# Clearing the expert row tables as attention begins instead of as the dense layer begins

## The chip, the cores and the metric

The kernel runs on one core of one Trainium2 chip. The metric is the device time of one execution in microseconds (us). Beside the time there is a profile of one execution, whose span runs from its first to its last instruction.

## What is computed

A decoder trunk of two layers on 256 tokens of width 1024. Layer 0 is gated DeltaNet linear attention and a dense SwiGLU (width 2816). Layer 1 is sliding-window attention with 16 query heads, 4 key/value heads and a learned sink per head, then a top-2-of-8 SwiGLU mixture of experts. After each of the four parts comes `layer_norm(ALPHA*x + h)`. What matters here, from the reference:

```python
    m = jnp.maximum(jnp.max(s, axis=-1, keepdims=True), sink)
    p = jnp.exp(s - m)
    p = p / (jnp.sum(p, axis=-1, keepdims=True) + jnp.exp(sink - m))
...
    top_v, top_i = lax.top_k(logits, TOP_K)
    top_w = jax.nn.softmax(top_v, axis=-1)
    gates = jnp.sum(jax.nn.one_hot(top_i, N_EXPERTS, dtype=jnp.float32) * top_w[..., None], axis=1)
    out = jnp.zeros_like(xt)
    for e in range(N_EXPERTS):
        h = xt @ w_gu[e]
        y = (jax.nn.silu(h[:, :D_EXPERT]) * h[:, D_EXPERT:]) @ w_down[e]
        out = out + gates[:, e:e + 1].astype(xt.dtype) * y
```

So attention needs the sinks for its very first maximum, and each expert works on the rows that the router sends to it.

## The kernel before, in words

The program is written engine by engine; each engine runs its list in order, and semaphores tie the lists together. The order within a list is the order of the code. The tokens are two blocks of 128.

**Weights.** All big weights pass as units of 1 MB (128 partitions x 2048 float32). SP loads unit j in two halves into one of six buffers `raw`, as soon as VectorE has cut unit j-6. ScalarE makes `hi` (a rounded copy, `cut_hi`, line 572), VectorE makes `lo = raw - hi` (`cut_lo`, line 946), and TensorE multiplies with both parts (most of it recorded as line 1529). The cuts run three units ahead of use. The units come in the order dense gate and up (U_GU), dense down (U_DOWN), shared key/value (U_KV), queries (U_Q), attention output (U_O), experts (U_MOE).

**The row tables.** `xe` and `ys` are tables in DRAM. For the experts, `xe` takes the rows of x sent to each expert by an indirect store, and `ys` their results; both have rows that nobody writes and that must be zero, so both are cleared once. Source of the zeros is `xTf[:, 0:4, :]`, an SBUF buffer set to zero by POOL (line 481). It gets its real content, the transposed x for the router, only behind the third norm: ScalarE's `xT_copy` and VectorE's `turned_sum` (line 1329).

**POOL's list around the change.** Behind the first norm (`norm(0)`): constants, the memset of xTf, the four clears (lines 484 to 487), more constants, then the small loads `wr` (router weights) and `gbT` (norm vectors). Then `norm(1)`, the norm behind the dense layer, which ends with the loads of `lng` and `lnb` (lines 397, 398). Then the memsets of `kT2` (lines 500, 501), the load of the sinks `sk` (line 503), the distances `dist`, and `wgb = wr * gbT` (line 515), for which a TensorE product in the midst of the key/value projection waits. All DMAs that POOL issues go through one queue of its own, q0; SP's go through q1.

**Attention.** TensorE alternates query projections and score products: queries(0), half of queries(1), scores(0), half of queries(1) and (2), scores(1), and so on. `scores(gi)` of TensorE waits for `sc_bias` gi, which VectorE's `scores(gi-1)` raises when it has taken the products out of PSUM. ScalarE's `exps` follow, then VectorE's `probs`, which TensorE transposes (line 1887). Ahead of its first `cut_lo` and `scores(0)` VectorE waits for the sinks and the distances:

```python
            dve.wait_ge(sink_here, 16)
            dve.wait_ge(consts, 4)
...
            cut_lo(U_Q + 0 + AHEAD)
            scores(0)
            cut_lo(U_Q + 1 + AHEAD)
            scores(1)
            probs(0)
```

`cut_lo(U_Q + 0 + AHEAD)` cuts unit U_Q+3. Behind attention the third norm follows, the router, and the experts. POOL waits for `xe_clear` before it stores rows in `xe`, and for `ys_clear` before the experts' results are gathered.

Of the kernel before, what the change touches and what calls it, by code (L numbers as in the profile page):

```python
# [25 lines left out]
P = 128  # L26
# [9 lines left out]
def trunk(nc, x_in, w_in, conv_w, a_log, dt_bias, norm_w, w_out, w_kv, w_q, sinks, w_o, w_gu, w_down,  # L36
          w_router, moe_gu, moe_down, ln_g, ln_b, out):
    _, T, D = x_in.shape
    NB = T // P
    KD = D // P  # L40
# [10 lines left out]
    E = w_router.shape[2]  # L51
# [24 lines left out]
    with ctx:  # L76
        def sb(name, shape, dt=F32, where=None):
            return (where or ctx).enter_context(nc.sbuf_tensor(name, shape, dt))

        def sem(name):  # L80
            return ctx.enter_context(nc.semaphore(name))
# [100 lines left out]
        xTf = sb("xTf", [P, KD, T])  # L182
# [66 lines left out]
        oneh_here, row_here, xe_clear, dispatched = (sem(n) for n in ("oneh_here", "row_here", "xe_clear", "dispatched"))  # L249
        gathered, xg_turned, xg_hi_here, xg_here = (sem(n) for n in ("gathered", "xg_turned", "xg_hi_here", "xg_here"))  # L250
        silu_here, act_here, ff_turned, h_hi, h_here = (sem(n) for n in ("silu_here", "act_here", "ff_turned", "h_hi", "h_here"))
        ys_clear = sem("ys_clear")
# [20 lines left out]
        xe = nc.dram_tensor("xe", [E * 2 * P, D], F32).ap()  # L273
        ys = nc.dram_tensor("ys", [E * 2 * P + P, D], F32).ap()
        NO_ROW = E * 2 * P
        xe_v = xe.rearrange("(e q s) d -> q e s d", q=2, s=P)
        ys_v = ys[0:NO_ROW, :].rearrange("(e q s) d -> q e s d", q=2, s=P)
# [12 lines left out]
        def xT_part(buf, s):  # L290
            return buf[:, 4 * (s % 2):4 * (s % 2) + 4, (s // 2) * P:(s // 2) * P + P]
# [81 lines left out]
        def _(pool):  # L373
            n = [0]

            def link(ins):
                n[0] += 1
                ins.then_inc(pool_chain, 1)
# [17 lines left out]
            def load_ln(layer, i):  # L396
                pool.dma_start(lng[:, :], ln_g[layer, i].partition_broadcast(P)).then_inc(ln_here, 16)
                pool.dma_start(lnb[:, :], ln_b[layer, i].partition_broadcast(P)).then_inc(ln_here, 16)
# [25 lines left out]
            def rsqrt(dst, src):  # L424
                return pool.tensor_tensor(dst, src, mhalf[:, 0:src.shape[1]], ALU.pow)  # L425
# [3 lines left out]
            for gr in range(4):  # L429
                s = slice(4 * gr, 4 * gr + 4)  # L430
# [3 lines left out]
            for gr in range(4):  # L434
                s = slice(4 * gr, 4 * gr + 4)
# [12 lines left out]
            for gr in range(4):  # L448
                s = slice(4 * gr, 4 * gr + 4)
# [17 lines left out]
            def norm(i):  # L467
                for b in range(NB):
                    pool.wait_ge(ln_var, 2 * i + b + 1)
                    rsqrt(lnrs[:, b:b + 1], lnve[:, b:b + 1]).then_inc(ln_rstd, 1)  # L470
                if i < 3:
                    pool.wait_ge(ln_done[0], i + 1)
                    pool.wait_ge(ln_done[1], i + 1)
                    load_ln((i + 1) // 2, (i + 1) % 2)
# [6 lines left out]
            link(pool.memset(xTf[:, 0:4, :], 0.0))  # L481
            settle()
            zeros = xTf[:, 0:4, :].rearrange("p k t -> p (k t)").unsqueeze(1)
            pool.dma_start(xe.rearrange("(r s) d -> s r d", s=P), zeros.to_broadcast([P, 2 * E, D])).then_inc(xe_clear, 16)
            pool.dma_start(ys_v[1].rearrange("e s d -> s e d"), zeros.to_broadcast([P, E, D])).then_inc(ys_clear, 16)
            pool.dma_start(ys[NO_ROW - 2 * P:NO_ROW - P, :], xTf[:, 0:4, :].rearrange("p k t -> p (k t)")).then_inc(ys_clear, 16)
            pool.dma_start(ys[NO_ROW:NO_ROW + P, :], xTf[:, 0:4, :].rearrange("p k t -> p (k t)")).then_inc(ys_clear, 16)
            link(pool.memset(last_place[:, :], float(P)))
            select(last_place[:, :], ALU.is_ge, 0.0, E - 2, [[-1, E]], 0)
            link(pool.iota(first_row[:, :], [[2 * P, E]], base=-1 - NO_ROW, channel_multiplier=0, allow_small_or_imprecise_dtypes=True))  # L490
# [4 lines left out]
            settle()  # L495
            pool.sem_inc(consts, 1)
            norm(1)


            link(pool.memset(kT2[64:128, :, 0, :], 0.0))  # L500
# [3 lines left out]
            for c, (base, op) in enumerate(((0, ALU.is_ge), (P, ALU.is_gt), (0, ALU.is_ge))):  # L504
                d = dist[:, c * P:(c + 1) * P]
# [61 lines left out]
        def _(act):  # L567
# [9 lines left out]
            def copy(dst, src, scale=1.0):  # L577
                return act.activation(dst, src, ACT.Copy, scale=scale)  # L578
# [74 lines left out]
            for gr in range(4):  # L653
                s = slice(4 * gr, 4 * gr + 4)
# [41 lines left out]
            for q in range(4, 4 * 7):  # L696
                s = slice(4 * (q % 4), 4 * (q % 4) + 4)
# [136 lines left out]
            def xT_copy(i):  # L834
                act.wait_ge(turned, 16 + i + 1)
                copy(xT_part(xTf, i), ps[:, 4 + i, :].rearrange("p (k t) -> p k t", k=4)).then_inc(xT_act, 1)

            xT_copy(0)
            xT_copy(1)
            act.wait_ge(xT_act, 2)  # L840
# [88 lines left out]
        def _(dve):  # L929
# [14 lines left out]
            def cut_lo(j, it=0):  # L944
                dve.wait_ge(hi_ready, j + 1 + PER_IT * it)
                dve.tensor_tensor(slot(lo, j), slot(raw, j), slot(hi, j).bitcast(F32), ALU.subtract).then_inc(lo_ready, 1)  # L946
# [156 lines left out]
            for gr in range(4):  # L1103
                s = slice(4 * gr, 4 * gr + 4)
# [6 lines left out]
            for gr in range(4):  # L1111
                s = slice(4 * gr, 4 * gr + 4)
# [212 lines left out]
            attended(3)  # L1325
            cut_lo(U_O + 1 + AHEAD)
            def turned_sum():
                dve.wait_ge(turned, 19)
                dve.tensor_copy(xT_part(xTf, 2), ps[:, 6, :].rearrange("p (k t) -> p k t", k=4)).then_inc(xT_dve, 1)
                dve.wait_ge(turned, 20)  # L1330

            norm(2, 0, U_O + 3, risen=turned_sum)

            each = [P, NB, E]
# [810 lines left out]
```

## Time and profile before

| | |
|---|---|
| median of 3 runs | 1269.55 us (1268.96 to 1269.56) |
| span of the profiled execution | 1267.7 us |
| TensorE (PE) busy | 1242.9 us, 98% |
| VectorE (DVE) busy | 1003.8 us, 79% |
| ScalarE (ACT) busy | 834.6 us, 66% |
| GpSimd (POOL) busy | 101.7 us, 8% |
| moved by DMA | 375.75 MB, mean 296 GB/s |

The profiled execution's own time is not among the three; its span stands 1.85 us below their median, and the start and end of an execution lie in that difference. Busy shares are means over stages with different limits. TensorE's end times are modelled. "Idle before" in a timeline names what the instruction waited for last.

### The profile page before, as it was taken

How to read it: one execution, taken by the hardware profiler on the slowest of the kernel's cores; microseconds unless marked ns; L12 is line 12 of the kernel's file. 1: busy time of each engine (PE TensorE's matmuls, PEld its weight loads, DVE VectorE, ACT ScalarE, POOL GpSimd, SP SyncE). 2: the span in 40 equal slices, each digit the busy share in tenths (PEclk: the TensorE clock that was granted, in tenths of full speed). 3: DMA queues.
4: the chain of work that ended last, by engine and by line, in shares of the span. 5: the costliest groups of instructions: out<-in, count | busy, mean ns of one | idle time of the engine just before them, and what ended most of it. 6: DMA issues, size and time to landing. Idle time of an engine off the chain costs nothing.

```text
span 1267.7 us, 16828 instructions
## 1 busy us (share of the span) xinstructions
PE 1242.9 (98%) x6731; PEld 1060.1 (84%) x6731; DVE 1003.8 (79%) x868; ACT 834.6 (66%) x842; POOL 101.7 (8%) x120
## 2 busy tenths in 40 slices
PE   9999999999999999999999999999999999999995
PEld 8998998888888978888888888888888888888884
DVE  6877846556646677988888888888888988898897
ACT  6795344545534474777777777777777777778773
POOL 4044212000001001300000000000000000001100
PEclk9999999999999999999999999999999999999998
DMA  9834013997554514999999999999999999999991
GB/s 315 271 148 137 2 34 125 413 348 243 181 186 163 192 43 166 333 397 397 389 393 389 390 384 371 391 388 372 389 387 377 386 391 378 382 380 363 390 397 74
DMA packets 189060, 375.75 MB, mean 296 GB/s; under 512 B 12321, under 2 KB 69777, under 8 KB 188977
## 3 DMA queue, kind: packets, MB, share of 16 engines
q1 hardware_dynamic: 179888, 345.02, 75.1%
q0 software_dynamic: 6928, 25.82, 5.4%
q10 hardware_dynamic: 2160, 3.79, 0.8%
q8 instruction: 55, 0.90, 0.3%
q14 instruction: 29, 0.23, 0.1%
HBM read 354.13 MB, written 20.45 MB: 295 GB/s over the span
## 4 chain that ended last, share of the span: by engine, by line
PE 88%; DMA 5%; DVE 3%; ACT 2%; POOL 1%; issue 1%; SPq 0%; DVEq 0%; POOLq 0%; ACTq 0%
PE ps L1529 85%; DMA raw<-in_ffn_w_gu 2%; DMA raw<-in_moe_w_gu 2%; PE ps L2041 1%; ACT hi L572 1%; DVE lo L946 1%; ACT ps L587 0%; PE ps L2034 0%; PE ps L1887 0%; PE ps L1660 0%; DMA x<-in_x 0%; DVE xT_both L954 0%; POOL lnrs L425 0%; SPq L306 0%; DVE x L1502 0%
## 5 line engine op out<-in xcount | busy, mean ns | idle before, releaser
L946 DVE TENSOR_TENSOR lo<-raw,hi 128x2048 fp32r<-128x2048 f32 x326 | 744.9, 2297 | 183.0 <-ACT hi L572 182.0
L572 ACT ACTIVATE hi<-raw 128x2048 fp32r<-128x2048 f32 x326 | 625.5, 1919 | 298.1 <-PE ps L1529 260.7
L1529 PE MATMUL ps<-hi,xg_hi 128*128 128x512 f32 x704 | 278.0, 395 | 0.1
L1529 PE MATMUL ps<-hi,xg_lo 128*128 128x512 f32 x704 | 274.6, 390 | 0.0
L1529 PE MATMUL ps<-lo,xg_hi 128*128 128x512 f32 x704 | 274.2, 389 | 0.0
L1529 PE MATMUL ps<-xT_both,hi 128*128 128x256 f32 (+1 forms) x896 | 222.9, 328 | 4.4 <-DVE xT_both L954 2.5
L1529 PE MATMUL ps<-xT_both,lo 128*128 128x256 f32 x624 | 175.8, 282 | 0.0
L1529 PEld LDWEIGHTS ps<-xT_both,hi 128*128 128x128 f32 x896 | 151.4, 191 | 20.1 <-issue 2.9
L1529 PEld LDWEIGHTS ps<-hi,xg_hi 128*128 128x128 f32 x704 | 132.2, 188 | 28.7 <-DVE lo L946 1.5
L1529 PEld LDWEIGHTS ps<-hi,xg_lo 128*128 128x128 f32 x704 | 132.1, 188 | 28.1
L1529 PEld LDWEIGHTS ps<-lo,xg_hi 128*128 128x128 f32 x704 | 132.3, 188 | 26.4
L1529 PEld LDWEIGHTS ps<-xT_both,lo 128*128 128x128 f32 x624 | 119.3, 191 | 0.0
L1529 PE MATMUL ps<-hi,hE_hi 128*128 128x512 f32 x352 | 111.1, 396 | 0.0
L1529 PE MATMUL ps<-hi,hE_lo 128*128 128x512 f32 x352 | 108.9, 390 | 0.0
L1529 PE MATMUL ps<-lo,hE_hi 128*128 128x512 f32 x352 | 108.9, 390 | 0.0
L1529 PEld LDWEIGHTS ps<-lo,hE_hi 128*128 128x128 f32 x352 | 66.1, 188 | 14.0
L1529 PEld LDWEIGHTS ps<-hi,hE_lo 128*128 128x128 f32 x352 | 66.1, 188 | 14.0
L1529 PEld LDWEIGHTS ps<-hi,hE_hi 128*128 128x128 f32 x352 | 64.0, 188 | 13.4 <-issue 1.1
L532 POOL DMA_DIRECT2D xg<-xe x7 | 3.8, 539 | 505.3 <-PE ps L2034 497.8
L1059 DVE SCALAR_TENSOR_TENSOR conv<-ps,cw,conv 128x255 f32<-128x255 f32 (+2 forms) x72 | 29.1, 471 | 10.2 <-ACT conv L613 10.1
L425 POOL TENSOR_TENSOR lnrs<-lnve,mhalf 128x1 f32<-128x1 f32 x8 | 7.0, 875 | 360.9 <-ACT lnve L590 360.9
L578 ACT ACTIVATE conv<-ps 128x512 f32<-128x512 f32 (+1 forms) x28 | 15.4, 564 | 29.3 <-PE ps L1529 29.3
(315 smaller groups left out, 1249.3 us busy)
## 6 DMA issues: line engine op xcount, KB each, us to landing
raw<-in_moe_w_gu SPq DMA_DIRECT2D x352, 512.0 KB, 7.2
raw<-in_moe_w_down SPq DMA_DIRECT2D x176, 512.0 KB, 7.1
raw<-in_ffn_w_gu SPq DMA_DIRECT2D x44, 512.0 KB, 8.1
raw<-in_dn_w_in SPq DMA_DIRECT2D x32, 512.0 KB, 8.9
raw<-in_ffn_w_down SPq DMA_DIRECT2D x22, 512.0 KB, 4.0
xe<-xTf POOLq DMA_DIRECT2D x1, 8192.0 KB, 29.0
raw<-in_dn_w_out SPq DMA_DIRECT2D x8, 512.0 KB, 3.9
ys<-xTf POOLq DMA_DIRECT2D x1, 4096.0 KB, 40.3
```

The source lines that it names most:

```text
L425: return pool.tensor_tensor(dst, src, mhalf[:, 0:src.shape[1]], ALU.pow)
L532: pool.dma_start(xg[:, :], xe_v[p][e]).then_inc(gathered, 16)
L572: act.activation(slot(hi, j), slot(raw, j), ACT.Copy).then_inc(hi_ready, 1)
L578: return act.activation(dst, src, ACT.Copy, scale=scale)
L946: dve.tensor_tensor(slot(lo, j), slot(raw, j), slot(hi, j).bitcast(F32), ALU.subtract).then_inc(lo_ready, 1)
L1059: dve.scalar_tensor_tensor(out=conv[:, t, d:T], in0=ps[:, t % 4, 0:T - d], scalar=cw[:, w:w + 1], in1=conv[:, t, d:T], op0=ALU.mult, op1=A ...
L1529: return pe.matmul(dst, lhsT, rhs, start=start, stop=stop)
L2041: last = pe.transpose(ps[:, 6 + c % 2, m * P:(m + 1) * P], actE[:, c % 2, m * P:(m + 1) * P], ident[:, :])
```

## The change

The four DMAs that clear `xe` and `ys` leave their place behind the memset of xTf and are issued behind `norm(1)`. Since the zeros are then read from xTf much closer to its reuse, the two engines that write it wait for the clears first.

```diff
             link(pool.memset(xTf[:, 0:4, :], 0.0))
             settle()
             zeros = xTf[:, 0:4, :].rearrange("p k t -> p (k t)").unsqueeze(1)
-            pool.dma_start(xe.rearrange("(r s) d -> s r d", s=P), zeros.to_broadcast([P, 2 * E, D])).then_inc(xe_clear, 16)
-            pool.dma_start(ys_v[1].rearrange("e s d -> s e d"), zeros.to_broadcast([P, E, D])).then_inc(ys_clear, 16)
-            pool.dma_start(ys[NO_ROW - 2 * P:NO_ROW - P, :], xTf[:, 0:4, :].rearrange("p k t -> p (k t)")).then_inc(ys_clear, 16)
-            pool.dma_start(ys[NO_ROW:NO_ROW + P, :], xTf[:, 0:4, :].rearrange("p k t -> p (k t)")).then_inc(ys_clear, 16)
             link(pool.memset(last_place[:, :], float(P)))
...
             norm(1)
+            pool.dma_start(xe.rearrange("(r s) d -> s r d", s=P), zeros.to_broadcast([P, 2 * E, D])).then_inc(xe_clear, 16)
+            pool.dma_start(ys_v[1].rearrange("e s d -> s e d"), zeros.to_broadcast([P, E, D])).then_inc(ys_clear, 16)
+            pool.dma_start(ys[NO_ROW - 2 * P:NO_ROW - P, :], xTf[:, 0:4, :].rearrange("p k t -> p (k t)")).then_inc(ys_clear, 16)
+            pool.dma_start(ys[NO_ROW:NO_ROW + P, :], xTf[:, 0:4, :].rearrange("p k t -> p (k t)")).then_inc(ys_clear, 16)
...
+            act.wait_ge(xe_clear, 16)
+            act.wait_ge(ys_clear, 48)
             xT_copy(0)
             xT_copy(1)
...
             def turned_sum():
+                dve.wait_ge(xe_clear, 16)
+                dve.wait_ge(ys_clear, 48)
                 dve.wait_ge(turned, 19)
```

POOL's list from the end of `norm(0)` to the load of the sinks, with the waits; first what stands in the kernel before:

```order
L481 MEMSET xTf 128x1024
L484 DMA xe<-xTf 128x16x1024 [waits pool_chain]
L485 DMA ys<-xTf 128x8x1024
L486 DMA ys<-xTf 128x1024
L487 DMA ys<-xTf 128x1024
L488 MEMSET last_place 128x8
L385 AFFINE_SELECT last_place<-last_place 128x8 [waits pool_chain]
L490 IOTA first_row 128x8
L491 DMA wr<-in_moe_w_router 128x8x8
L493 DMA gbT<-in_ln_g 128x8x1
L494 DMA gbT<-in_ln_b 128x8x1
```

The four clears stand ahead of wr and gbT in POOL's list and in its queue. Now the changed kernel, POOL's list behind `norm(1)`:

```order
L397 DMA lng<-in_ln_g 128x1024 [waits ln_done1,ln_done0]
L398 DMA lnb<-in_ln_b 128x1024
L494 DMA xe<-xTf 128x16x1024
L495 DMA ys<-xTf 128x8x1024
L496 DMA ys<-xTf 128x1024
L497 DMA ys<-xTf 128x1024
L500 MEMSET kT 64x4x256
L501 MEMSET kT 64x4x256
L503 DMA sk<-in_sw_sinks 128x16 [waits pool_chain]
```

They now stand ahead of the memsets of kT2 and of sk; wr and gbT have no clears ahead of them any more.

VectorE's list in the changed kernel, where it waits for the sinks (its order is the one of before):

```order
L1267 COPY vB<-ps 128x512 [waits unit_used]
L1269 TENSOR_REDUCE wsum<-ps 128x16 [waits wsum_mm]
L1270 TENSOR_SCALAR wsum<-wsum 128x8 [waits dve_chain]
L948 TENSOR_TENSOR lo<-raw,hi 128x2048 [waits hi_ready,consts,sink_here]
L1282 SCALAR_TENSOR_TENSOR sS<-dist,ps 128x128 [waits sc_mm]
```

Nothing moved there; the wait for sk (`sink_here`) stands in front of the cut of U_Q+3 and of scores(0).

## Rows read from the trace of the kernel before

**Rows 1.** Head of the page.
```profile
span 1267.7 us, 16828 instructions
```
**Rows 2.** The chain that ended last, dense layer: start us, us, what.
```profile
233.94 29.68 DMA raw<-in_ffn_w_gu
```
**Rows 3.** Timeline of PE, dense layer: start us, us, instruction, idle before it.
```profile
267.94 0.50 PE L1529 MATMUL ps<-xT_both,hi 128*128 128x512 f32 x1 [1.90 <-DVE lo L946]
```
**Rows 4.** Stretches: length; busy us of PE, PEld, DVE, ACT, POOL; clock, DMA share, GB/s.
```profile
217.60:261.60 44.00, 44.00 (x256) 38.46 (x255) 23.75 (x19) 16.98 (x17) 6.23 (x10) 1.00 1.03 401
...
268.00:274.00 6.00, 6.00 (x25) 5.18 (x26) 5.62 (x6) 5.42 (x6) 0.00 (x0) 0.72 1.10 349
...
300.00:340.00 40.00, 40.00 (x233) 35.28 (x232) 25.99 (x22) 20.94 (x23) 0.00 (x0) 1.00 0.53 189
...
411.00:456.00 45.00, 43.90 (x367) 40.80 (x365) 33.79 (x61) 25.31 (x64) 3.78 (x8) 1.00 0.50 169
```
**Rows 5.** DMA issues: count, KB each, median us from issue to landing.
```profile
xe<-xTf POOLq DMA_DIRECT2D x1, 8192.0 KB, 29.0
ys<-xTf POOLq DMA_DIRECT2D x1, 4096.0 KB, 40.3
...
wr<-in_moe_w_router POOLq DMA_DIRECT2D x1, 32.0 KB, 41.6
...
gbT<-in_ln_b POOLq DMA_DIRECT2D x1, 4.0 KB, 42.2
sk<-in_sw_sinks POOLq DMA_DIRECT2D x1, 8.0 KB, 4.6
```
**Rows 6.** Timeline of POOL behind the first norm.
```profile
217.60 1.20 POOL L484 DMA_DIRECT2D xe<-xTf  x1 [0.30 <-POOL xTf L481]
...
220.75 0.14 POOL L488 MEMSET last_place<- 128x8 f32 x1
...
221.21 0.94 POOL L491 DMA_DIRECT2D wr<-in_moe_w_router  x1
...
223.03 0.88 POOL L494 DMA_DIRECT2D gbT<-in_ln_b  x1
```
**Rows 7.** Timeline of POOL behind the second norm.
```profile
408.20 0.95 POOL L500 MEMSET kT<- 64x1024 f32 x1
...
410.44 0.54 POOL L503 DMA_DIRECT2D sk<-in_sw_sinks  x1 [0.30 <-POOL kT L501]
...
414.86 0.55 POOL L515 TENSOR_TENSOR wgb<-wr,gbT 128x64 f32<-128x64 f32 x2 [0.18 <-POOL dist L385]
```
**Rows 8.** Timeline of PE: the wgb product, scores(1), first turned probabilities.
```profile
415.46 0.49 PE L1529 MATMUL ps<-wgb,ones 128*128 128x128 f32 x2 [1.10 <-POOL wgb L515]
...
438.16 2.22 PE L1529 MATMUL ps<-kT,qT 64*128 64x256 f32 x16
...
448.12 1.04 PE L1887 MATMUL ps<-ident,sS 128*128 128x128 f32 x8
```
**Rows 9.** Timeline of SP's DMA queue: a pair of loads, one unit.
```profile
426.06 0.89 SPq L306 DMA_DIRECT2D raw<-in_moe_w_gu  x2
```
**Rows 10.** Timeline of DVE, from the router's sums to the first probabilities.
```profile
426.99 0.17 DVE L1268 TENSOR_SCALAR wsum<-wsum 128x8 f32<-128x8 f32 x1
...
432.52 0.29 DVE L1280 SCALAR_TENSOR_TENSOR sS<-dist,ps 128x128 f32<-128x128 f32 x1
...
434.31 0.41 DVE L1282 SCALAR_TENSOR_TENSOR sS<-dist,ps 128x256 f32<-128x256 f32 x1
...
437.89 2.29 DVE L946 TENSOR_TENSOR lo<-raw,hi 128x2048 fp32r<-128x2048 f32 x1 [0.83 <-ACT hi L572]
...
440.42 0.29 DVE L1280 SCALAR_TENSOR_TENSOR sS<-dist,ps 128x128 f32<-128x128 f32 x1 [0.24 <-PE ps L1529]
...
445.91 1.22 DVE L1300 TENSOR_TENSOR sS<-sS,sinv 128x1024 f32<-128x1024 f32 x1
```
**Rows 11.** Timeline of ACT: the first copy into xTf.
```profile
490.47 1.06 ACT L578 ACTIVATE xTf<-ps 128x512 f32<-128x512 f32 x2
```

## The prediction

> **What bounds the kernel now.** I read the page first: a span of 1267.7 us [rows 1]. The chain of work that ended last is almost all TensorE, so only what makes TensorE stand or run at its lower clock costs time. I then looked for where a DMA stands in that chain. It does once in the dense layer: a load of ffn_w_gu that took 29.68 us to land, then the two cuts of that weight unit (ScalarE, then VectorE) [rows 2]. At its end TensorE stands for 1.90 us [rows 3]. That is much less than 29.68 us, because weights loaded ahead covered the rest. Afterwards the granted clock averages 0.72 over the next 6 us (part of it at 1.2 GHz instead of 2.4) [rows 4]. In the undisturbed dense layer TensorE is busy throughout and weights come at 189 GB/s; during the clears the core moves 401 GB/s in all; in attention only 169 GB/s [rows 4].
>
> The clears are 8192 and 4096 KB [rows 5] and two of 128 x 1024 float32, 512 KB each: 13.63 MB. Over 44.0 us the core moved 17.6 MB, so only some 4.0 MB, about 90 GB/s, was left for weights, half of what the dense layer needs. The stall is the clears' doing.
>
> **What is removed.** Without clears the dense layer keeps its 189 GB/s. The standing time goes, 1.90 us, and so does the loss by the clock, (1 - 0.72) x 6 = 1.7 us: a gain of 3.6 us. As a lower end I take the 1.90 us alone.
>
> **What is moved, on POOL.** The four issues took from 217.60 to 220.75 us, 3.15 us [rows 6]. They now stand directly behind the loads of lng and lnb, where the first memset of kT2 started at 408.20 us, so all up to wgb, which starts at 414.86 us, comes 3.15 us later [rows 7]. TensorE already waits 1.10 us for wgb at 415.46 us [rows 8]; there is no slack, so it reaches scores(1), now at 438.16 us, at 441.3 us. Alone this would cost 3.15 us. Moved off the other place, wr and gbT land earlier; nothing waits for them before 414.86 us, so that is worth nothing.
>
> **What is moved, on the DMA queue.** This is the dear part. The load of the sinks, sk, is issued by POOL at 410.44 us and lands in 4.6 us today [rows 5, 7]. After the change it stands behind 13.63 MB in POOL's own queue. The trace shows what this does to a small transfer: wr, 32 KB, issued right behind the clears at 221.21 us, took 41.6 us, and the last gbT, 4 KB, issued at 223.03 us, took 42.2 us [rows 5, 6]. They landed 45.2 and 47.6 us after the first clear's issue. sk takes the place that wr had, so I put it at 408.20 + 45.2 = 453.4 us. The weight traffic beside it is alike: four units of 1 MB are issued between 411 us and the pair at 426.06 us [rows 9], 3.15 us later in the changed kernel, as much as passed beside the clears in the dense layer; more are not issued while VectorE stands, since SP waits for its cuts.
>
> VectorE waits for sk behind the sums for the router (426.99 us) and ahead of the cut of weight unit U_Q+3 and of scores(0). Queued behind that wait are, on VectorE, the cut and the scores; behind those, ScalarE's exps(0) and TensorE's scores(1), which needs sc_bias 1. Today scores(0) starts at 432.52 us and ends at 434.31 + 0.41 = 434.72 us, 3.4 us before TensorE asks [rows 10]. From 453.4 us on:
> - the cut, 2.29 us, and 0.14 us to the next start: scores(0) begins at 455.8 us and ends 2.20 us later, at 458.0 us. TensorE resumes at 458.1 us, having stood since 441.3 us.
> - On VectorE the first probabilities are ready at 445.91 + 1.22 = 447.13 us today, 14.61 us after scores(0) began. Of this 0.83 and 0.24 us are idle, which fall away when the work has piled up: 13.54 us, hence 469.4 us [rows 10].
> - TensorE turned these probabilities at 448.12 us, 9.96 us after scores(1) [rows 8]. Now 458.1 + 9.96 = 468.1 us, and 1.7 us more if the lower clock after the stop costs what it did after the 1.90 us stop: 469.8 us. It is a little later than VectorE's 469.4 us.
>
> So the rest of attention comes 469.8 - 448.12 = **21.7 us later**. The 3.15 us on POOL are inside this, being over before TensorE stops at 441.3 us. From here both chains shift together.
>
> **What is added as waits.** ScalarE waits for all clears ahead of the first copy into xTf, 490.47 us today [rows 11], VectorE a little later. The clears are done before sk, at about 453 us, and that place moves to 512 us: cost nothing, cover about 59 us. That also covers the dispatch of rows.
>
> **Bounds of the landing of sk.** At the early end the clears have the whole 401 GB/s: 34.0 us, sk at 442.2 us, 11.2 us less. At the late end sk does as the last gbT did, 2.4 us more; the 1 MB of lng and lnb, issued closer ahead than in the dense layer, adds up to 2.5 us; a lower clock that lasts twice as long adds 1.7 us: 6.6 us in all. I stay with wr, which stood in just this place behind the same four transfers.
>
> What a page says of the rate: the Trainium skill, "DMA: Bandwidth & Descriptors", section on the anatomy of one DMA on the gpsimd path, gives 2.0 us plus the bytes at 436 GB/s. By it the clears take 33.3 us, sk lands at 441.5 us, and the sum would be 1275.8 us. The trace disagrees where others load as well: the xe clear of 8192 KB took 29.0 us [rows 5], and the page would give 21.2 us.
>
> **The sum.** 1267.7 - 3.6 + 21.7 = 1285.8 us of span. The median of the runs, 1269.55 us, stands 1.85 us above the span, so I predict **1287.7 us**. Early end 1276.5 us, late end 1294.3 us; the lower end of the gain (1.7 us less) lies within these.
>
> **Rivals.**
> - *sk is not held by the clears.* Then only the POOL shift counts: 1269.55 - 3.6 + 3.15 = 1269.1 us, no change. For it: the loads on SP's queue went on beside the clears. Against it: wr and both gbT, all on POOL's queue, landed only once the clears had. The Trainium skill ("DMA: Bandwidth & Descriptors", queues, rings and completion order) says that a later DMA of a queue may complete before an earlier one; by that the time would be this 1269.1 us. wr speaks against it here. Chance 0.06.
> - *Faster.* It takes sk landing by 436.7 us (441.3 less 2.29, 0.14 and 2.20 us), the point from which it costs TensorE nothing, and four issues on POOL shorter than their 3.15 us, so that wgb is on time: 1269.55 - 3.6 = 1266.0 us. 13.63 MB by 436.7 us would be 478 GB/s, more than any row. Chance 0.02.
> - *Slower still.* The clears starve the loads of w_o and of the first expert as they starved ffn_w_gu. They get 90 GB/s, and some 4 MB are asked for; the first cut that needs them stands behind TensorE's stop, after 469 us, so I see no second stall. If there is one like the first, 10 us with the clock: 1297.7 us. Chance 0.06.
> - *That the clears do not move*: the order of POOL's instructions shows that they do.
>
> **How the numbers follow.** My forecast has a chance of 0.86, its early and late landings included. A measurement of this kernel can tell 0.2%, 2.5 us, from no change. Faster 0.02, same 0.06, slower 0.86 + 0.06 = 0.92. The range is the forecast's own, 1276.5 to 1294.3 us; it leaves out all the rivals, 0.14.
>
> **What would show it.** Right: no DMA in the chain between 215 and 300 us and TensorE full there; sk landing over 30 us after its issue; VectorE idle for some 20 us ahead of the cut before scores(0), and TensorE for about 17 us ahead of scores(1), with a lower clock behind; no idle time by the new waits. Wrong: sk landing in 5 us, or TensorE standing at xTf or in the first expert.

## The result, and the profile after

The changed kernel takes 1292.38 us (median of 4 runs, 1290.96 to 1294.17) against 1269.26 us for the kernel before on the same chip: ratio 1.019, interval 1.0174 to 1.0206. It is 23.1 us slower; 18 us were forecast, and the 1287.7 us predicted are 4.7 us too low. Head of the page and two issue rows, kernel after:

```profile
span 1290.1 us, 16830 instructions
...
PEclk9999999999999889999999999999999999999998
...
xe<-xTf POOLq DMA_DIRECT2D x1, 8192.0 KB, 36.2
...
wr<-in_moe_w_router POOLq DMA_DIRECT2D x1, 32.0 KB, 5.8
```

The span grew by 22.4 us from [rows 1]. wr, no longer behind the clears, lands in 5.8 us and not 41.6 [rows 5]. POOL's timeline behind the second norm, kernel after, answers to [rows 6, 7]:

```profile
404.68 0.61 POOL L397 DMA_DIRECT2D lng<-in_ln_g  x1 [2.09 <-DVE x L1000]
405.29 0.55 POOL L398 DMA_DIRECT2D lnb<-in_ln_b  x1
405.82 1.19 POOL L494 DMA_DIRECT2D xe<-xTf  x1
...
409.00 0.95 POOL L500 MEMSET kT<- 64x1024 f32 x1
...
411.25 0.55 POOL L503 DMA_DIRECT2D sk<-in_sw_sinks  x1 [0.29 <-POOL kT L501]
...
413.98 2.60 POOL L515 TENSOR_TENSOR wgb<-wr,gbT 128x64 f32<-128x64 f32 x2 [0.19 <-POOL dist L385]
```

The clears push the memsets back by 3.18 us (405.82 to 409.00), against 3.15 us predicted. The second norm ends earlier than before, at 404.68 and not at 407.02 us. The chain that ended last, kernel after (start us, us, what):

```profile
411.25 43.36 DMA sk<-in_sw_sinks
...
454.63 2.29 DVE lo L948
...
459.19 12.48 PE ps L1533 x80
471.67 0.87 PE ps L1891 x8
```

No load of ffn_w_gu stands in it any more [rows 2]. In its place stand the 43.36 us that 8 KB of sinks wait behind the clears. What this did to the two engines stands in their timelines (VectorE, then TensorE, kernel after; to compare with [rows 8, 10]):

```profile
429.61 0.17 DVE L1270 TENSOR_SCALAR wsum<-wsum 128x8 f32<-128x8 f32 x1
454.63 2.29 DVE L948 TENSOR_TENSOR lo<-raw,hi 128x2048 fp32r<-128x2048 f32 x1 [24.86 <-DMA sk<-in_sw_sinks]
456.84 0.28 DVE L1282 SCALAR_TENSOR_TENSOR sS<-dist,ps 128x128 f32<-128x128 f32 x1
...
458.62 0.42 DVE L1284 SCALAR_TENSOR_TENSOR sS<-dist,ps 128x256 f32<-128x256 f32 x1
...
468.96 1.22 DVE L1302 TENSOR_TENSOR sS<-sS,sinv 128x1024 f32<-128x1024 f32 x1
```

```profile
416.63 0.80 PE L1533 MATMUL ps<-wgb,ones 128*128 128x128 f32 x2 [4.60 <-POOL wgb L515]
...
459.19 4.08 PE L1533 MATMUL ps<-kT,qT 64*128 64x256 f32 x16 [18.33 <-DVE sS L1284]
```

VectorE stands 24.86 us, cuts the unit and takes scores(0); 0.15 us after that TensorE starts scores(1), having stood for 18.33 us since 440.86 us. Stretches of the kernel after (columns as in [rows 4]):

```profile
405.82:454.60 48.78, 30.20 (x234) 29.32 (x234) 12.50 (x13) 12.86 (x14) 9.73 (x16) 0.85 0.98 388
...
410.00:420.00 10.00, 5.40 (x33) 5.20 (x33) 4.97 (x6) 3.30 (x5) 5.64 (x10) 0.83 1.02 405
...
459.00:471.00 12.00, 11.81 (x76) 10.56 (x77) 11.72 (x25) 8.04 (x30) 0.00 (x0) 0.78 0.48 166
```

The 22.4 us of span add up like this, measured between loads of lng, which mark the ends of the norms:

| stretch | before | after | difference |
|---|---|---|---|
| start to norm 0 | 214.49 | 215.91 | +1.4 |
| norm 0 to norm 1 (dense layer) | 192.53 | 188.77 | -3.8 |
| norm 1 to norm 2 (attention) | 89.63 | 115.43 | +25.8 |
| norm 2 to the end | 771.05 | 769.99 | -1.1 |

The first row has nothing to do with the change: the later kernels' profiles, all with the same program up to there, show 214.4 to 215.0 us, and once 215.90.

### The profile page after: what moved, and what is told of

The parts are those of the page before. It is cut to its first block, busy times and chain, and to the rows that moved or that the text cites. A ratio compares the mean times of both kernels' runs of the same rounds, so it can differ in the third digit from the quotient of the medians.

```text
span 1290.1 us, 16830 instructions
## 1 busy us (share of the span) xinstructions
PE 1245.9 (97%) x6731; PEld 1063.7 (82%) x6731; DVE 1004.0 (78%) x868; ACT 834.4 (65%) x842; POOL 102.5 (8%) x120
## 4 chain that ended last, share of the span: by engine, by line
PE 91%; DMA 4%; DVE 2%; ACT 1%; POOL 1%; issue 0%; SPq 0%; DVEq 0%; POOLq 0%; ACTq 0%
PE ps L1533 87%; DMA sk<-in_sw_sinks 3%; PE ps L2045 1%; ACT ps L587 0%; PE ps L2038 0%; PE ps L1891 0%; PE ps L1664 0%; DMA x<-in_x 0%; PE ps L1544 0%; POOL lnrs L425 0%; DVE x L1506 0%; DVE x L1000 0%; POOL DT L451 0%; DVE x L1010 0%; DVE xT_both L956 0%
```

## The experiments

The theory: sk, in POOL's own queue, lands only when the clears ahead of it have. VectorE waits for sk, and TensorE for VectorE. Rivals: the clears' mere traffic beside attention (starved weights, slow loads), POOL's later instructions (wgb), the added waits. All measured times are medians, all ratios against the kernel before on the same chip (1267.96 us for the first four, 1268.22 us for the next four, 1268.14 us for the last two and for the repeat of the third). Diffs are against the changed kernel, unless said otherwise.

### sk ahead of the clears, same queue

```diff
             norm(1)
+            pool.dma_start(sk[:, :], sinks[0].partition_broadcast(P)).then_inc(sink_here, 16)
             pool.dma_start(xe.rearrange("(r s) d -> s r d", s=P), zeros.to_broadcast([P, 2 * E, D])).then_inc(xe_clear, 16)
...
-            pool.dma_start(sk[:, :], sinks[0].partition_broadcast(P)).then_inc(sink_here, 16)
```

> The changed kernel with one line moved: the load of the sinks is issued by POOL ahead of the four clears instead of behind them. Theory (sk is held by 13.63 MB ahead of it in POOL's own queue): sk lands in 4 to 8 us, VectorE does not wait for it, TensorE does not stand ahead of scores(1). What is left is the gain in the dense layer (3.8 us) and the four issues ahead of wgb (TensorE stands about 4.6 us there instead of 1.1, and its clock may drop behind it): 1269 to 1271 us. Rival (the 16 DMA engines are simply full while the clears run, whatever the order): sk still takes 15 us or more and the time stays above 1280 us.

Measured: 1269.48 us (11 runs), ratio 1.0014 [1.0005, 1.0024]. The issue rows of this kernel:

```profile
xe<-xTf POOLq DMA_DIRECT2D x1, 8192.0 KB, 36.8
...
ys<-xTf POOLq DMA_DIRECT2D x2, 512.0 KB, 52.2
...
sk<-in_sw_sinks POOLq DMA_DIRECT2D x1, 8.0 KB, 5.2
```

One line moved takes the ratio from 1.019 to 1.0014, some 22 of the 23 us, with the same bytes beside the same work. TensorE's stop ahead of scores(1) is gone; its wait for wgb (2.3 us) is what is left. So the order within the queue makes the loss; traffic and the new waits do not. What the four issues on POOL cost when no long stop hides them shows here too: norm 1 to norm 2 takes 92.45 us in this profile, 2.8 us more than before, 1.2 us of it the longer wait for wgb (2.3 against 1.10 us) and the rest the clock, 0.83 over 410 to 420 us (1.7 us).

### sk on ScalarE's queue

```diff
-            pool.dma_start(sk[:, :], sinks[0].partition_broadcast(P)).then_inc(sink_here, 16)
...
             cut_hi(U_KV + AHEAD)
+            act.dma_start(sk[:, :], sinks[0].partition_broadcast(P)).then_inc(sink_here, 16)
```

> The changed kernel, but sk is issued by ScalarE on its own queue, behind its third cut for the key/value projection, so some 6 us after the first clear, while the clears run. Only the queue differs from the changed kernel. Theory: sk lands in 5 to 15 us, as the weights on SP's queue did (median 9.0, at most 15.1 us in this stretch), and the time is 1269 to 1271 us. Rival (contention, not the queue): sk takes 30 us or more, as in the changed kernel, and the time is above 1285 us.

Measured: 1268.26 us (10 runs), ratio 0.9997 [0.9988, 1.0006]. sk's row:

```profile
sk<-in_sw_sinks ACTq DMA_DIRECT2D x1, 8.0 KB, 8.1
```

Issued at 411.1 us, 6.3 us behind the first clear (5.4 us in the changed kernel) and in the midst of the clears, sk lands in 8.1 us on another queue. Against the 4.6 us of before, sharing the 16 DMA engines with 13.63 MB costs it some 3.5 us; standing behind them in one queue costs 39. The time is a little below the 1269 to 1271 us expected; the kernel before is 1.3 us faster here than the 1269.26 us from which they were worked out. Norm 1 to norm 2 takes 91.85 us, 2.2 us more than before, by the same two causes as in the kernel with sk first: 0.65 us more wait for wgb and the clock behind it (0.83 over 412 to 422 us).

### The clears behind wgb

```diff
             norm(1)
-            pool.dma_start(xe.rearrange("(r s) d -> s r d", s=P), zeros.to_broadcast([P, 2 * E, D])).then_inc(xe_clear, 16)
...
                                    ALU.mult).then_inc(wg_here, 1)
+            pool.dma_start(xe.rearrange("(r s) d -> s r d", s=P), zeros.to_broadcast([P, 2 * E, D])).then_inc(xe_clear, 16)
...
             norm(2)
```

> The changed kernel with the four clears issued behind wgb, so behind sk and behind all that POOL must do for attention. Theory: sk lands in about 5 us, wgb is on time, the dense layer keeps its gain of 3.8 us: 1269.3 - 3.8 = 1265.5 us, 1264.5 to 1266.5 us. The clears, issued at about 413 us, land in some 48 us, by 461 us, before the first copy into xTf at about 487 us: no idle time by the new waits. Rival (clears starve the loads of w_o and of the first expert wherever they run beside them): TensorE stands again between 440 and 520 us and the time is 1268 us or more.

Measured: 1266.3 us (11 runs), ratio 0.9985 [0.9976, 0.9994]. The same kernel was measured again in a later session:

> The clears behind wgb once more, on the same chip as the two others, to compare them: 1.7 us less than the kernel before, 1 to 3 us.

1267.76 us (11 runs), ratio 0.9999 [0.9991, 1.0008]. (The three clears of ys move with that of xe.) In both profiles sk lands in time and TensorE waits 1.1 us for wgb, as before the change. The two medians put the gain between nothing and 0.15%; it is not the 3.6 us that the profile of before promises. The first time lies inside its range (1264.5 to 1266.5 us) only by luck: the range was set against a kernel before of 1269.3 us, which takes 1267.96 us here, so the gain is 1.7 us and not 3.8. The repeat, expected at 1 to 3 us less, shows 0.4 us. Why one profile can't tell this stands below, under the two paces.

### The added waits alone

Against the kernel before:

```diff
+            act.wait_ge(xe_clear, 16)
+            act.wait_ge(ys_clear, 48)
             xT_copy(0)
...
             def turned_sum():
+                dve.wait_ge(xe_clear, 16)
+                dve.wait_ge(ys_clear, 48)
```

> The kernel before with only the added waits (ScalarE and VectorE wait for the clears ahead of xTf). All theories: the clears have landed over 220 us earlier, so no idle time and 1269.3 us, within 1 us. If the waits themselves cost, over 1271 us.

Measured: 1268.52 us (10 runs), ratio 1.0003 [0.9994, 1.0012]: they cost nothing. Its profile holds a miss of another kind. The clears load the dense layer as in the kernel before (a load of ffn_w_gu with 21.54 us in the chain), yet TensorE stands for 0.1 us there, the clock does not fall, and norm 0 to norm 1 takes 190.21 us.

### Only the ys clears in attention

```diff
             zeros = xTf[:, 0:4, :].rearrange("p k t -> p (k t)").unsqueeze(1)
+            pool.dma_start(xe.rearrange("(r s) d -> s r d", s=P), zeros.to_broadcast([P, 2 * E, D])).then_inc(xe_clear, 16)
...
             norm(1)
-            pool.dma_start(xe.rearrange("(r s) d -> s r d", s=P), zeros.to_broadcast([P, 2 * E, D])).then_inc(xe_clear, 16)
```

> The changed kernel, but the clear of xe (8.39 MB) goes back to the start of the dense layer; only the three clears of ys (5.24 MB) stay behind norm(1), ahead of sk. If sk waits for the bytes ahead of it, and only its landing past about 437 us costs time, sk lands some 17 to 22 us after the first clear, by about 428 us, and TensorE does not stand ahead of scores(1). The dense layer has 29 us of clears instead of 45, which the weights loaded ahead nearly cover. Time: that of the kernel before, within 2.5 us. Rival (any clear ahead of sk costs in proportion to its bytes, without a threshold): 5.24 of 13.63 MB of the loss, some 9 us more than before.

Measured: 1271.89 us (10 runs), ratio 1.0027 [1.0015, 1.0039]. VectorE's wait, and TensorE's two:

```profile
431.42 2.29 DVE L948 TENSOR_TENSOR lo<-raw,hi 128x2048 fp32r<-128x2048 f32 x1 [7.78 <-DMA sk<-in_sw_sinks]
```

```profile
PE ps L1533 <- DVE sS L1284: 1.3, 1, 1.3
PE ps L1891 <- DVE sS L1302: 0.9, 1, 0.9
```

5.24 of 13.63 MB ahead of sk, 38% of the bytes, give some 3.4 us and not 38% of 23 us, which would be 9. It is still more than was expected (no stop of TensorE, within 2.5 us): sk lands 27.1 us after the first clear, not 17 to 22. VectorE stands for 7.8 us and TensorE for 2.2: the loss has the threshold of which the prediction spoke. Without its 1.26 us of waiting TensorE would have started scores(1) at 434.71 us; from sk's landing to that start it takes 4.55 us, so a landing by 430.2 us would have been free, and sk landed at 431.4. This profile is of the fastest of the ten runs, 4.1 us below their median: in it attention is 3.0 us longer than before and the dense layer 3.8 us shorter, so it does not show where the median's 3.4 us come from in full. And the 8.39 MB of xe in the dense layer cost that layer nothing: norm 0 to norm 1 takes 188.76 us.

### More bytes ahead of sk

An extra clear of 3584 KB of rows that the experts write later, behind the second one (with the waits for ys_clear raised to 64):

```diff
             pool.dma_start(ys_v[1].rearrange("e s d -> s e d"), zeros.to_broadcast([P, E, D])).then_inc(ys_clear, 16)
+            pool.dma_start(ys_v[0][0:E - 1].rearrange("e s d -> s e d"), zeros.to_broadcast([P, E - 1, D])).then_inc(ys_clear, 16)
```

> The changed kernel with a fifth clear of 3584 KB (3.67 MB, rows of ys that the experts write later) behind the second, so ahead of sk. If the bytes ahead of sk set its landing, it comes 9 us later (3.67 MB at 400 GB/s) to 13 us later (at the 3.6 us per MB that sk has now), and the whole kernel as much: 9 to 13 us above the changed kernel's 1292.4 us. Rival (a fixed cost of being behind on the queue, whatever the bytes): no more than 2 us.

Measured: 1300.61 us (4 runs), ratio 1.0259 [1.0242, 1.0276].

```profile
462.06 2.29 DVE L949 TENSOR_TENSOR lo<-raw,hi 128x2048 fp32r<-128x2048 f32 x1 [32.25 <-DMA sk<-in_sw_sinks]
```

sk lands 57.2 us after the first clear, 8.4 us later than the 48.8 of the changed kernel, and the kernel is some 8.8 us slower than it (0.0069 of 1268 us), just under the 9 to 13 us expected. Past the threshold every microsecond of landing is one of time, 2.3 us for a MB (8.4 us for 3.67 MB).

### More bytes in the dense layer

The same extra clear, in the kernel before:

> The kernel before with the same fifth clear of 3.67 MB, in the dense layer. While clears run there, weights come at 90 GB/s instead of the 189 that TensorE uses; 9 to 13 us more of that put TensorE back by 5 to 7 us. So 1273 to 1276 us, and a bound on how dear clears are there once the weights loaded ahead are used up. Rival (the dense layer hides the clears): 1270 us or less.

Measured: 1277.62 us (4 runs), ratio 1.0084 [1.0067, 1.0101]. That is 10.7 us over the kernel before, where 4 to 7 us were expected.

```profile
PE ps L1530 <- DVE hf L1249: 8.9, 1, 8.9
```

With 8.39 MB (xe alone, above) the dense layer loses nothing, with 13.63 MB TensorE stands 1.90 us [rows 3] or 0.1, with 17.3 MB 8.9 us. So here too the weights loaded ahead are a cover with an edge, and the kernel before sits just on it.

### lng and lnb behind sk

```diff
                     pool.wait_ge(ln_done[1], i + 1)
-                    load_ln((i + 1) // 2, (i + 1) % 2)
+                    if i != 1:
+                        load_ln((i + 1) // 2, (i + 1) % 2)
...
             pool.dma_start(sk[:, :], sinks[0].partition_broadcast(P)).then_inc(sink_here, 16)
+            load_ln(1, 0)
```

> The changed kernel with the loads of lng and lnb (1 MB) issued behind sk instead of ahead of the clears. sk landed 48.8 us after the first clear, not 45.2 us as wr had. If the 1 MB of lng and lnb beside the clears makes the difference, sk lands 2 to 3 us sooner and the time falls by as much, to about 1290 us. If it is the weight units that SP asks for at that moment, it stays within 1 us of the changed kernel.

Measured: 1292.27 us (4 runs), ratio 1.0195 [1.0178, 1.0212]. sk lands 47.9 us after the first clear, not 48.8: issuing the 1 MB of norm vectors behind it brings back 0.9 of the 3.6 us by which it landed later than predicted. The time does not fall clear of the noise (1.0195 against 1.0190). The 2 to 3 us expected did not come, but the experiment took away less than it seems. By queue, over the landing of sk (packets, MB, busy share), in this kernel and then in the changed one:

```profile
q0 software_dynamic: 3590, 14.28, 77.6%
q1 hardware_dynamic: 1408, 4.19, 21.7%
```

```profile
q0 software_dynamic: 3712, 14.69, 76.4%
q1 hardware_dynamic: 1408, 4.19, 21.3%
```

q0 is POOL's queue, and 13.63 MB of it are the clears. The changed kernel moves 1.06 MB more than them on q0, which is lng and lnb. This kernel still moves 0.65 MB more, although lng and lnb are issued behind sk: only 0.4 MB, worth 1.0 us at 386 GB/s, left the stretch, and sk landed 0.9 us sooner. So the 3.6 us that are left to explain are not all the weights' doing; the sum stands below.

### The clears in the midst of the dense layer

```diff
-            norm(1)
+            pool.wait_ge(unit_used, U_DOWN - 5)
             pool.dma_start(xe.rearrange("(r s) d -> s r d", s=P), zeros.to_broadcast([P, 2 * E, D])).then_inc(xe_clear, 16)
...
+            norm(1)
```

> The clears are issued in the middle of the dense layer, when POOL sees that 17 of the 22 gate and up units are used, at about 310 us. From 302 us on SP loads units of w_down, whose rows are 4 KB long like those of the clears, where those of w_gu are 1 KB. Theory: the 16 DMA engines take turns between the queues row by row, so that short rows get the smaller share: w_gu got 90 GB/s beside the clears and w_o far more (2 MB in 15 us). Then w_down gets about half of 400 GB/s, 200 GB/s, against 189 GB/s that TensorE uses: no DMA in the chain, sk and wgb as in the kernel before, and 1.4 to 3.8 us less than the kernel before. Rival (weights get 90 GB/s beside clears whatever their rows): TensorE stands at about 350 us as it did at 266 us, and the time is that of the kernel before or more.

Measured: 1268.59 us (12 runs), ratio 0.9996 [0.9986, 1.0007]: 0.5 us less than before, where 1.4 to 3.8 were expected. That no load starves came out as expected. The issue rows, and the stretch in which the clears run:

```profile
raw<-in_ffn_w_down SPq DMA_DIRECT2D x22, 512.0 KB, 8.8
xe<-xTf POOLq DMA_DIRECT2D x1, 8192.0 KB, 37.8
```

```profile
312.41:370.00 57.59, 57.59 (x291) 48.75 (x290) 31.44 (x24) 27.41 (x24) 3.11 (x4) 1.00 1.02 410
```

TensorE is full through all of it. 57.59 us at 410 GB/s are 23.6 MB, so 10.0 MB of others passed beside the clears, 173 GB/s; early in the dense layer others got 17.6 - 13.6 = 4.0 MB in 44 us, 90 GB/s [rows 4]. The loads differ: ffn_w_gu is read in pieces of 1 KB, ffn_w_down in rows of 4 KB. (16 of the 20 loads issued in the stretch are of ffn_w_down, the others of w_kv_shared.) That a queue with longer rows gets more beside the clears fits; no run here tries it with nothing else changed, and since TensorE uses only 189 GB/s there [rows 4] and never stands, 173 GB/s may be all that was asked for and not the most that the queue could have got.

### More filler products in the router

In the kernel with the clears behind wgb:

```diff
-            full(6, 6)
+            full(9, 6)
```

> The kernel with the clears behind wgb, and nine instead of six filler products while VectorE ranks the router's logits (their results are not used). In the profile of that kernel TensorE's clock fell to 1.2 GHz for about 3.5 us behind the three stops of the third norm and the router (0.9 us in the 4 us of the largest), which the kernel before did not show: 1.6 us lost. If less standing keeps the clock up, this kernel is 0.5 to 1.6 us faster than the one without the filler. If the clock's fall there is a matter of chance from run to run, the two medians agree within 0.5 us.

Measured: 1267.2 us (11 runs), ratio 0.9995 [0.9985, 1.0005]. The clock did not fall in its profile. It did not fall in the second profile of the kernel without the filler either (below), so this decides nothing.

## Why the prediction was right, and what it had wrong

The path was right and the size of one term on it was not.

**The mechanism** came out as written: sk behind the clears, VectorE ahead of the cut (24.86 us), TensorE ahead of scores(1) (18.33 us, "some 17"), resuming at scores(0)'s end. That the wait is the queue's is shown twice: by sk ahead of the clears, and by sk in another queue.

**POOL shift.** 3.15 us predicted, 3.18 measured. wgb's start moved by less, since one operation on the distances between took 0.29 us after and 1.99 before; its end moved by more, 3.55 us, since its own two operations took 2.60 us and not 0.55 (2.63 us with lng and lnb behind sk, 0.55 in the other profiles); TensorE stood 4.60 us there, and the clock was 0.83 over 410 to 420 us. All of it ends before the long stop and is inside it, as the prediction had it: it paid 4.25 us of standing (1.10 + 3.15) and no fall of the clock there.

**Landing of sk: the term that was mis-sized.** It was put 45.2 us after the first clear's issue, like wr's; it was 48.8, +3.6 us. "The weight traffic beside it is alike" is the step that failed. Over wr's 45.2 us the core moved 396 GB/s, 17.9 MB; over sk's 48.78 us it moved 388 GB/s, 18.9 MB. The 1.0 MB more is worth 2.6 us, the rate 0.9 us. By queue over wr's 45.2 us, kernel before (the changed one stands under lng and lnb behind sk):

```profile
q0 software_dynamic: 3639, 14.23, 78.7%
q1 hardware_dynamic: 3672, 3.65, 24.9%
```

The four units that the prediction counted are the 4.19 MB on q1 in the changed kernel, so their number was right. Wrong was "as much as passed beside the clears in the dense layer": there it was 3.65 MB of weights, 0.54 MB less, and the rest of that traffic was the tail of lng and lnb (14.23 less 13.63 MB of clears is 0.6 MB, wr's 32 KB in it). In the changed kernel lng and lnb are issued directly ahead of the clears and pass whole, 1.06 MB, 0.46 MB more; this the prediction had put among its bounds and not into the sum. So the 3.6 us are 1.4 us of weights, 1.2 us of lng and lnb and 0.9 us of rate (estimates from these bytes at 388 GB/s).

The same sum holds in three kernels. Taking off the clears, others moved 5.3 MB in the changed kernel (18.9 - 13.6), 5.2 MB with ys alone (27.1 us at 385 GB/s, less 5.24 MB) and 5.3 MB with the extra clear (57.2 us at 395 GB/s, less 17.3 MB), each time four units of weights and the two norm vectors. So in attention sk lands when the clears and some 5.3 MB have passed at 385 to 395 GB/s. The 5.3 MB have an end because VectorE stands and SP waits for its cuts: with sk ahead of the clears, VectorE goes on, others move 8.3 MB (54.9 us at 400 GB/s) and the last clear lands 54.9 us after the first issue. Nobody waits for it there.

**TensorE behind the stop.** From scores(1) to the first turned probabilities it took 12.31 us, 0.65 more than the 9.96 + 1.7 predicted; the granted clock was 0.78 over 459 to 471 us, that is, some 5 of the 12 us at 1.2 GHz and the rest at 2.4. The 1.7 us taken from the short stop [rows 4] were a little low for a stop ten times as long.

**The dense gain.** 3.6 us predicted, 3.8 in the two profiles. But the timed medians show less: the kernels whose clears leave the start of the dense layer and hold nobody up (behind wgb, twice, with more filler, in mid layer) come out 0.1 to 1.9 us faster than before, not 3.6. The 1.90 us stop and the clock were read from one profile, and the profile with the waits alone shows 0.1 us for the same work. An estimate of the usual gain, from the middle of these, is 1 us, which takes 2 to 3 us off what was set against the 21.7 us.

**Added waits**: nothing, as said. **Slower still**: no second stall. In the issue rows the loads of w_o (raw<-in_sw_w_out), asked for beside the clears, take 11.9 us instead of 5.1, and TensorE never stands for them.

**In sum**: the changed kernel came out 23.1 us slower, against 18.1. In the profile the terms close: 18.1, landing +3.6, scores +0.65, dense gain -0.2, the later start +1.4 and the experts -1.1, which nearly cancel, are 22.4 us of span. The medians do not close as well: attention's 25.8 us less a dense gain of 1 us would be 24.8 us. That is inside the interval of the ratio (22.1 to 26.1 us); that the 23.1 us come so near the profile's 22.4 is partly luck.

## What to carry to other kernels

A DMA queue that holds megabytes is a wall for the small load behind it. Before moving bulk transfers, look at what is issued next on that same queue and who waits for it, then put that load ahead of them or on another queue. Where the bulk goes beside other work matters less: it was hidden behind wgb, in mid dense layer and up to 8.39 MB at its start alike. And a loss that comes from lateness has an edge: work out the latest landing that costs nothing, and do not scale by bytes. Last, a stop of 2 us in one profile is not yet 2 us in the median; look for it in a second trace before it is booked as a gain.

## What the runs showed that was not expected

**TensorE has two paces at the full granted clock.** The dense layer's products, 282 to 332 us, by form, of the kernel with the clears behind wgb, first and second profile (count, busy us, mean ns):

```profile
L1533 PE MATMUL ps<-xT_both,hi 128*128 128x512 f32 x145 | 50.3, 391 | 0.0
L1533 PE MATMUL ps<-xT_both,lo 128*128 128x256 f32 x145 | 40.6, 280 | 0.0
```

```profile
L1533 PE MATMUL ps<-xT_both,hi 128*128 128x512 f32 x143 | 50.6, 399 | 0.0
L1533 PE MATMUL ps<-xT_both,lo 128*128 128x256 f32 x142 | 39.9, 281 | 0.0
```

The wide product takes 391 ns or 399, and there are fewer of them in 50 us; TensorE does not stand, the clock is 1.00 in both, and both are the same program. Norm 0 to norm 1 is 188.80 us in the first and 191.13 us in the second. It falls in two groups over all kernels without a stop there: 188.76 to 188.80 us in seven profiles (391 to 394 ns), 191.11 to 191.14 us in three (399 ns: the repeat, lng and lnb behind sk, clears in mid layer). The kernel with the waits alone went at 399 ns before its 0.1 us stop and at 391 behind it. What sets the pace is open. It is worth 2.3 us, more than the question whether moving the clears gains 0.1%, and it is one reason why a single profile could not answer it.

**A stop of 0.9 us may or may not cost the clock.** The stretch of the third norm and the router, in the same two profiles:

```profile
495.00:499.00 4.00, 4.00 (x24) 3.73 (x24) 2.86 (x4) 0.00 (x0) 0.00 (x0) 0.71 0.63 236
```

```profile
497.00:501.00 4.00, 4.00 (x34) 3.73 (x34) 2.85 (x4) 0.45 (x1) 0.00 (x0) 1.00 0.69 249
```

Behind the same short stops (the longest 0.9 us) the clock fell in the first and not in the second: from the load of lng to the first store of rows it took 31.80 us against 30.15.
